# Intra-chunk scores of the prompt heads: merged into one masked tile by predicated copies, in alternating PSUM banks

## What is computed

```python
def step(s, inp):
    qb, kb, vb, gb = inp
    G = jnp.cumsum(gb, axis=1)
    o_inter = jnp.einsum('bthk,bhkv->bthv', qb * jnp.exp(G), s)
    diff = G[:, :, None] - G[:, None, :]
    decay = jnp.exp(jnp.where(causal, diff, -jnp.inf))
    scores = jnp.einsum('bthk,btshk->btsh', qb, decay * kb[:, None])
    o_intra = jnp.einsum('btsh,bshv->bthv', scores, vb)
    ...
    return s_new, o_inter + o_intra
```

## Time and profile before

| | us |
|---|---|
| median of three runs | 1762.51 (1758.94 to 1763.24) |
| the profiled execution | 1763.91 |
| its span in the profile | 1760.8 |
| TensorE busy | 1703.6 |
| VectorE busy | 1280.1 |
| loop over the twelve heads, layer 0 | about 127 to 201 |
| the same, layer 1 | about 629 to 699 |

### The profile page before, as it was taken

How to read it: one execution, slowest core, us unless ns; L and a number is a source line. 1 busy time by engine, 2 the same in 40 slices (tenths; PEclk the granted TensorE clock), 3 DMA queues, 4 the chain that set the end, 5 groups by cost and what they waited for, 6 DMA issues and landing times.

```text
span 1760.8 us, 23377 instructions
## 1 busy us (share of the span) xinstructions
PE 1703.6 (97%) x9626; PEld 1483.1 (84%) x9626; DVE 1280.1 (73%) x1203; ACT 1038.9 (59%) x942; POOL 96.7 (5%) x85
## 2 busy tenths in 40 slices
PE   8999989999999999889999999999999999999997
PEld 7988878999999978678888888888888888788886
DVE  6635755444357347559988898988889888888897
ACT  4443433333234344257777777777777777777776
POOL 2001120000000010203200000000000000000200
PEclk9997989999999989899999999999999999999999
DMA  9549263443554413259999999999999999999994
GB/s 300 164 147 280 59 191 118 146 137 114 144 161 132 156 46 77 60 181 367 401 394 397 396 368 390 366 384 394 358 384 375 371 396 388 318 392 370 371 395 182
DMA packets 272616, 474.07 MB, mean 269 GB/s; under 512 B 41578, under 2 KB 103266, under 8 KB 272504
## 3 DMA queue, kind: packets, MB, share of 16 engines
q1 hardware_dynamic: 266432, 452.37, 72.1%
q10 hardware_dynamic: 3368, 12.75, 2.2%
q0 software_dynamic: 2704, 7.39, 1.5%
HBM read 454.69 MB, written 29.84 MB: 275 GB/s over the span
## 4 chain that ended last, share of the span: by engine, by line
PE 90%; DVE 5%; ACT 2%; issue 2%; DMA 1%; POOL 0%; DVEq 0%; ACTq 0%
PE ps L1715 16%; PE ps L1716 16%; PE ps L2359 11%; PE ps L1710 9%; PE ps L1711 9%; PE ps L2380 5%; PE ps L1809 4%; PE ps L2245 3%; PE ps L1926 2%; PE ps L1904 1%; PE ps L2263 1%; DVE spL L1595 1%; PE ps L2398 1%; PE ps L2207 1%; DMA ring<-in_w_exp_in_dram 1%
## 5 line engine op out<-in xcount | busy, mean ns | idle before, releaser
L1595 DVE TENSOR_TENSOR spL<-ring,spH 128x2048 fp32r<-128x2048 f32 x336 | 767.3, 2292 | 99.5 <-ACT spH L963 96.7
L963 ACT ACTIVATE spH<-ring 128x2048 fp32r<-128x2048 f32 x336 | 643.0, 1916 | 129.8 <-PE ps L2359 70.6
L1715 PE MATMUL ps<-spH,XH 128*128 128x512 f32 x896 | 354.3, 395 | 2.0 <-issue 2.0
L1716 PE MATMUL ps<-spH,XL 128*128 128x512 f32 x896 | 350.2, 391 | 0.0
L1046 DVE TENSOR_TENSOR spL<-ring,spH 128x2048 fp32r<-128x2048 f32 (+1 forms) x74 | 158.8, 2146 | 182.3 <-ACT spH L658 182.1
L1710 PE MATMUL ps<-hnH,spH 128*128 128x320 f32 x928 | 277.4, 313 | 4.0 <-DVE hnL L1061 2.2
L1711 PE MATMUL ps<-hnL,spH 128*128 128x320 f32 x928 | 275.6, 311 | 0.0
L658 ACT ACTIVATE spH<-ring 128x2048 fp32r<-128x2048 f32 (+1 forms) x74 | 133.4, 1803 | 187.6 <-PE ps L2245 73.6
L2359 PE MATMUL ps<-spL,XH 128*128 128x512 f32 x896 | 241.2, 391 | 0.9 <-DVE spL L1595 0.9
L2359 PEld LDWEIGHTS ps<-spL,XH 128*128 128x128 f32 x896 | 168.6, 188 | 37.7 <-DVE spL L1595 1.8
L1715 PEld LDWEIGHTS ps<-spH,XH 128*128 128x128 f32 x896 | 168.6, 188 | 36.2 <-issue 2.4
(11 more groups left out here) (363 smaller groups left out, 1775.1 us busy)
## 6 DMA issues: line engine op xcount, KB each, us to landing
ring<-in_w_exp_in_dram SPq DMA_DIRECT2D x224, 1024.0 KB, 8.1
ring<-in_w_exp_out_dram SPq DMA_DIRECT2D x112, 1024.0 KB, 8.5
ring<-in_w_in_dram SPq DMA_DIRECT2D x28, 1024.0 KB, 5.3
ring<-in_w_ffn_in_dram SPq DMA_DIRECT2D x22, 1024.0 KB, 5.1
token_rows<-token_rows ACTq DMA_DIRECT2D x1, 11776.0 KB, 39.8
ring<-in_w_ffn_out_dram SPq DMA_DIRECT2D x16, 704.0 KB, 4.6
ring<-in_w_out_dram SPq DMA_DIRECT2D x8, 1024.0 KB, 5.1
out_dram<-ring SPq DMA_DIRECT2D x32, 256.0 KB, 2.7
```

The costliest lines, as they stand in the source:

```text
L963: A(esplit(j)[0], src, ACT.Copy).then_inc(S("hi_done"), 1)
L1595: V.tensor_tensor(lo, eslot(j)[0], hi.bitcast(F32), ALU.subtract).then_inc(S("split_done"), 1)
L1715: mm(out, x[0], w, start=start, stop=False)
L1716: return mm(out, x[1], w, start=False, stop=False)
```

## The change

The masks, the PSUM layout, the VectorE step `masked` and two places of TensorE's loop change.

- `scores` writes one bank, 2 for even heads and 3 for odd ones. At every low level only the columns of the queries (the right blocks, half of them: function `later`) are computed, so a prompt head has 5 x 64 + 128 = 448 columns in place of 768. The weights stay the whole level of Y. The diagonal and the blocks of the high levels share 128 columns and are laid behind the low levels.
- `masked` builds one tile SC of 128x128 (64x64 for tile 2): one multiply with a mask for the diagonal and the high levels, then one predicated copy for each low level, which lays its scores over it where its mask is set. Each of these six instructions (four for tile 2) waits for the one before it on VectorE.
- `output` is one matmul with SC (and line 1931 as before).
- `scores` waits for `masked` of two heads before, not of one.
- TensorE's loop issues `scores` of this head right behind the exponents of the next, and `output` of the head before comes later, behind `turn_said` and `ask`, for every head alike.

```diff
+def later(x, v):
+    return x.rearrange("p (g r b) -> p g r b", r=2, b=1 << v)[:, :, 1]
...
                 def masked(t, h):
                     dve.wait_ge(S("sc_mm"), j + 1)
                     if j >= 2:
                         dve.wait_ge(S("o_mm"), j - 1)
-                    SCv = flat(SCb[h % 2])[:, 0:((LOW if t < 2 else nl) + 1) * n]
-                    if t < 2:
-                        V.tensor_tensor(SCv, ps[:, 2:4, :].rearrange("p b n -> p (b n)")[:, 0:(LOW + 1) * n], tabv("mask"),
-                                        ALU.mult).then_inc(S("sc_done"), 1)
-                    else:
-                        V.tensor_tensor(SCv[0:n], ps[0:n, 2, 0:(nl + 1) * n], tabv("ms")[0:n], ALU.mult
-                                        ).then_inc(S("sc_done"), 1)
+                    low = LOW if t < 2 else LS
+                    sc = SCb[h % 2][0:n, 0:n]
+                    raw_sc = ps[0:n, 2 + h % 2]
+                    mask = tabv("mask" if t < 2 else "ms")[0:n]
+                    own(V.tensor_tensor(sc, raw_sc[:, low * n // 2:low * n // 2 + n], mask[:, 0:n], ALU.mult))
+                    for v in range(low):
+                        mine = mask[:, n + v * n // 2:n + (v + 1) * n // 2].bitcast(I32)
+                        ins = V.copy_predicated(later(sc, v), mine.rearrange("p (g b) -> p g b", b=1 << v),
+                                                raw_sc[:, v * n // 2:(v + 1) * n // 2].rearrange("p (g b) -> p g b", b=1 << v))
+                        if v < low - 1:
+                            own(ins)
+                    ins.then_inc(S("sc_done"), 1)
...
                 def scores(t, h):
                     pe.wait_ge(S("y_done2"), j + 1)
-                    if j:
-                        pe.wait_ge(S("sc_done"), j)
-                    full = LOW if t < 2 else nl
-                    for v in range(full + 1):
-                        at_ = (v * n) % 512
-                        out = ps[0:n, 2 + (v * n) // 512, at_:at_ + n]
-                        if v < full:
-                            m = mm(out, flat(Yb[h % 2])[:, v * n:(v + 1) * n],
-                                   flat(Yb[h % 2])[:, v * n:(v + 1) * n], start=True, stop=True)
-                        else:
-                            m = mm(out, kT[:, h, o:o + n], qT[:, h, o:o + n], start=True, stop=True)
+                    if j >= 2:
+                        pe.wait_ge(S("sc_done"), j - 1)
+                    full, bank = LOW if t < 2 else nl, 2 + h % 2
+                    at_ = full * n // 2
+                    m = mm(ps[0:n, bank, at_:at_ + n], kT[:, h, o:o + n], qT[:, h, o:o + n], start=True, stop=True)
+                    for v in range(full):
+                        y = flat(Yb[h % 2])[:, v * n:(v + 1) * n]
+                        m = mm(ps[0:n, bank, v * n // 2:(v + 1) * n // 2].rearrange("p (g b) -> p g b", b=1 << v),
+                               y, later(y, v), start=True, stop=True)
...
                 def output(t, h):
-                    top = LOW if t < 2 else nl
-                    for v in range(top + 1):
-                        m = mm(out, vtk_of(t)[0:n, h * P:(h + 1) * P], flat(SCb[h % 2])[0:n, v * n:(v + 1) * n],
-                               start=v == 0, stop=v == top and t != 1)
+                    m = mm(out, vtk_of(t)[0:n, h * P:(h + 1) * P], SCb[h % 2][0:n, 0:n], start=True, stop=t != 1)
...
                 for j, (t, h) in enumerate(HEADS):
-                    if h == H - 1:
-                        output(*HEADS[j - 1])
                     if j + 1 < len(HEADS):
                         exponents(*HEADS[j + 1])
+                    scores(t, h)
                     if (t, h) in TOLD_AT:
                         turn_said(0, TOLD_AT[t, h])
                     if (t, h) in ASK_AT:
                         ask(0, ASK_AT[t, h])
-                    if j and h < H - 1:
+                    if j:
                         output(*HEADS[j - 1])
                     if (t, h) in SEQ_AT:
                         sample_state(SEQ_AT[t, h])
                     if h == 0 and j:
                         turn_values(t)
-                    scores(t, h)
```

More of the change, by code:

```diff
@@ L89, in constants @@
         "id": np.eye(P), "ones": np.ones((P, P)),
-        "mask": np.concatenate([mp[:, :LOW], mp[:, LOW:].sum(1, keepdims=True)], 1).reshape(P, -1), "ms": ms.reshape(NS, -1), "seq": seq, "turn": turn,
+        "mask": np.concatenate([mp[:, LOW:].sum(1)] + [mp[:, v, (i >> v) % 2 == 1] for v in range(LOW)], 1),
+        "ms": np.concatenate([ms[:, LS]] + [ms[:, v, (i[:NS] >> v) % 2 == 1] for v in range(LS)], 1),
+        "seq": seq, "turn": turn,
         "iota": np.tile(i[None, :], (P, 1)), "before": (i[:, None] < i[None, :]),
@@ L248, in build @@
         sc0 = cursor[0]
-        SC = put("SC", [P, LV + 1, P])
+        SC = put("SC", [P, P])
+        cursor[0] += 3584
         qG = put("qG", [P, H, NS])
@@ L268, in build @@
         Yb = [Y, put("Y1", [P, LV, P], offset=hn0 + 4 * 1024)]
-        SCb = [SC, put("SC1", [P, LV + 1, P], offset=hn0 + 11 * 1024 + 512)]
+        SCb = [SC, put("SC1", [P, P], offset=hn0 + 11 * 1024 + 512)]
         ea = put("ea", [P, NSQ * NH], offset=hn0 + 15 * 1024 + 512)
@@ L1910, in scores @@
                         for s0 in range(0, n, 2 * b):
-                            m = mm(ps[s0:s0 + b, 2 + (full * n) // 512, at_ + s0 + b:at_ + s0 + 2 * b],
+                            m = mm(ps[s0:s0 + b, bank, at_ + s0 + b:at_ + s0 + 2 * b],
                                    flat(Yb[h % 2])[:, v * n + s0:v * n + s0 + b],
```

## The result

The changed kernel takes 1776.78 us (median; 1762.92 to 1781.17), the kernel before 1762.51 (1758.94 to 1763.24). The ratio is 1.0099, with a 95% interval of 1.007 to 1.0128: slower by 1%, or some 17 us, where the prediction had 1754.1 and a range up to 1768. The profiled execution is the shortest of the five, 1762.92 us with a mean granted clock of 0.972; the other four took 1776.04 to 1781.17, with a clock of 0.965 or 0.966. So the trace shows what changed in kind, but about 14 us less of it than the median has.

A forecast was written before the change was run, and what follows sets the result against it. TensorE was taken to bound the kernel (busy 97% of the span, 90% of the chain). Savings of 5.2 us in layer 0 and 4.6 in layer 1, 9.8 off 1763.9, gave 1754.1 us; range 1748 to 1768.

The forecast's parts named there:

- Outputs: TensorE's output matmuls: twelve records become two, about 0.30 us, saving 1.12 us per prompt head.
- Scores: TensorE's low-level scores: halved columns gain nothing, because ten records stay at about 0.112 us each.
- Masked: VectorE's masking step: six dependent instructions take 1.59 us against 0.92, 0.67 more per prompt head; bounds 1.2 and 1.9.
- Rival 3: VectorE's masking: a predicated copy takes 0.35 us, so the total is 1762 to 1763, no change; chance 0.08.
- Order: TensorE's loop: scores no longer wait for the previous head's masking, but three other waits lose their cover.
- the three covers: Work hiding TensorE's waits: for low_gates at a tile's first exponents, for turn_keys (0.4 us), for sample_state (0.67 later).
- The pause: TensorE standing before the first exponents of tile 1, waiting for VectorE's low_gates: 3.5 us.
- The sum of 9.8: Total saved in the loops over heads: 5.2 us in layer 0 and 4.6 in layer 1.
- Clock as before: TensorE's granted clock in the loops over heads stays as profiled; with copies of 0.15 to 0.3 us, chance 0.53.
- Rival 1: TensorE's clock drops in the loops: 3 to 11 us lost, chance 0.22; longer and slower, up to 1782 us, 0.12.
- one row of 5.19 of 6.8 us busy at a clock of 1.00: Profile stretch 205.6 to 212.4, large and small matmuls mixed, cited as evidence against a clock drop.
- What follows the loop hangs on its end alone, so both shifts reach the end: After the loops: the experts' part is TensorE at its limit, so both layers' savings, 9.8 us, reach the total.

The follow-up runs named there:

- e2_old_order: Changed kernel with TensorE's loop in the order of the kernel before (output where it was, scores last): 1779.81 us, ratio 1.0141 to the kernel before.
- a1_again: The changed kernel run once more without any edit: 1774.51 us, against 1758.95 for the kernel before (ratio 1.0082).
- e12: Changed kernel with the old buffer addresses and all 128 columns moved in low-level scores, pause left in: 1754.73 us, ratio 1.0003 to the kernel before.
- e4: Changed kernel with a 1,664-byte hole behind the table of constants, which restores the old buffer addresses: 1771.84 us, ratio 1.0087 to the kernel before.
- e6: Changed kernel with old buffer addresses and the next tile's gates turned earlier, their low part earlier for the last tile: 1752.04 us, ratio 0.9967 to the kernel before.
- e7: Changed kernel with old buffer addresses, the next tile's gates taken earlier and full 128 columns in low-level scores: 1747.36 us, ratio 0.9945 to the kernel before.
- e9: Kernel before with only a 384-byte hole behind the table of constants, no instruction changed: 1765.36 us against 1759.97, ratio 1.004.
- e3: Changed kernel with useless matmuls filling the pauses before the first exponents of tiles 0 and 1: 1761.83 us, ratio 1.0018 to the kernel before.
- e10: The kernel of e7 run again, on one chip with the kernel before: 1745.21 us against 1757.13, ratio 0.9919.
- e13: Changed kernel with the 1,664-byte hole ahead of the experts' last three buffers only, restoring just their old addresses: 1773.71 us, ratio 1.0105 to the kernel before.
- e1: Changed kernel with low-level scores moving all 128 columns again, unneeded halves overwritten: 1763.32 us, ratio 1.0037 to the kernel before.

## Why the prediction was wrong, point by point

- **Outputs:** right. Two records, 0.39 to 0.49 with the end of the last one; the next group starts 0.22 to 0.32 later.
- **Scores:** right. Ten records of 64 columns start 1.16 us before the next group, against 1.11 to 1.22 for 128 columns. The figure of the Trainium skill weighed there ("TensorE: Matmul & The Clock Gate", Back-to-back issue gap) is given for matmuls by themselves. The same section says that in a stream of weight loads and matmuls both set the spacing. This case is such a stream, so its 0.116 a record isn't the contradiction that I made of it; I had read the figure outside its case.
- **Masked:** 1.72 instead of 1.59; a copy of 64 columns is 0.25 with 0.03 to the next, in the bounds. Rival 3 (0.35 a copy) is out.
- **Order:** the three covers went as told. The pause was 4.50 at tile 1 (predicted 3.5) and 1.41 at tile 0 (1.4); `turn_keys` waited 0.27 (0.4); rounds of tile 1 are 4.65 (4.7). The pause is longer because TensorE came to it sooner: it stopped at 158.6 and VectorE had the gates ready at 163.0, not at 165.8. e2_old_order has the order by itself as a gain of 5.3 us, clock and all, hardly beyond the noise.
- **The sum of 9.8:** of the right sign and size at equal clock, as far as the estimates go. a1_again lies 15.6 us above the kernel before. Its median execution has 49 us more at half clock (0.966 against 0.980), at 0.4 some 20 us, and the addresses take 5.4 to 5.7. What is left for the layout is 15.6 - 20 - 5.5, about -10; at 0.5, the most that the clock can cost, it is -14. The traces give the same bounds: at 800 us the changed kernel is 3.8 us ahead with 20.5 us more at the low clock in the mixers, which is -12 at 0.4 and -14 at 0.5.
- **"Clock as before":** this is the step that failed. The forecast rested on it with 0.53. Rival 1 had the mechanism, its place (164.6; it was 163.3) and even the point from which it decides, about 11 us in each layer; the typical execution lost some 25 a layer. The weight was wrong: 0.34 for a lost clock, and 0.12 of it for a loss as long as this. I had named two reasons for it, a pause of 3.5 us and scores that leave half the array idle, and e12 with e4, e6 and e7 shows that each costs by itself (7.4 us and 4.7) and that the two cost 24.5 together. Against it I put one row of 5.19 of 6.8 us busy at a clock of 1.00; one short stretch with its own neighbours was too little to hold a clock over 47 us. I also priced it by one stretch of 10 us; there are two in each layer, and the second, from 187.2 on, stands where no pause is.
- **"What follows the loop hangs on its end alone, so both shifts reach the end":** failed as well, by 5.5 us. The matmuls of the experts' part aren't a fixed 227.8 ns: a shorter table of constants moved their operands, and they became 229.6 (e4, e9). No rival had this.

So the loss is, by these estimates, the sum of -10 to -14 from the layout, +20 to +25 from the clock and +5.5 from the addresses. The addresses are shown by runs that change nothing else. That the clock is the larger part is shown by e3, which saves no wait and no work; the split between clock and layout isn't measured to better than these bounds.

## What to carry to other kernels

Columns taken off matmuls whose time is set by their weights save nothing here and cost clock: 4 to 5 us by themselves, 11 to 17 beside a pause. Look for the new pause first and move what it waits for, and leave the useless columns in. When a table or buffer changes its size, keep the addresses behind it (a hole costs nothing) or measure the shift by itself. With these mended the change gains 0.5% to 0.8% on the kernel before (e7: 0.9945; e10: 0.9919); as made, it costs 1%.

## What the runs showed of the hardware that I had not expected

- Matmuls that are otherwise the same run at 227.8 or 229.7 ns from start to start by the address of their operands alone; 384 bytes more did it in the kernel before (e9), as did 1,664 fewer in the changed one, and e13 shows more than one buffer in it. The Trainium skill ("SBUF — State Buffer", Who interferes with whom) says that PE and ACT never wait on anyone; these runs show TensorE's pace depend on where buffers lie, while VectorE splits weights and DMA lands them beside it. Whether TensorE waits for another engine there, or its two own reads (weights and moving tile) meet, stays open; in the second case the page's sentence would stand. VectorE alone isn't it: from the kernel before to e9 the spacing grows from 227.9 to 230.0 ns where VectorE and ScalarE are busy throughout, and from 227.4 to 228.8 where VectorE is idle and ScalarE busy (some 150 records). It comes in single records: of the products of spH with XH 5% are 235 ns or more apart in the kernel before and 25% in e9.
- The clock can couple edits that look independent: halved columns cost 4.7 us without the pause, and 17.1 (e4 and e12) or 11.2 (a1 and e1) beside it.
- Executions of one kernel differ in how long the clock is low, and in time: a1_again from 1761.86 us at 0.972 to 1780.06 at 0.966. The 0.006 are 21 us at half clock, which explain at most 11 of the 18 us; the rest is open. One profile of such a kernel is one draw; the mean clock of all executions belongs beside it.
